# A fused pair of hybrid blocks on one core: the recurrence's keys made by another engine, and two chunks of the first mixer copied and turned earlier

## The chip, the cores and the metric

The kernel runs on 1 core of one Trainium2 chip. The metric is device time in microseconds (us) of one execution. Engines are TensorE (PE in the rows; PEld is its weight load), VectorE (DVE), ScalarE (ACT), GpSimd (POOL) and SyncE (SP), which issues the DMAs here.

## The reference, cut to what matters

A sequence of 256 tokens with 1024 features passes four layers, each of which is a feed-forward part, a mixer and a feed-forward part. Layers 0 and 1 have the first kind of mixer, layers 2 and 3 the second. Everything is float32.

```python
# mixer of layers 0 and 1: differential, stick-breaking and block attention
proj = h @ w_in
dq, dk = partial_rope(dq, cos, sin), partial_rope(dk, cos, sin)   # differential attention
p = softmax(causal(dq @ dk.T * scale)); w = p[:, :, 0] - lam * p[:, :, 1]

# mixer of layers 2 and 3: a gated recurrence and dilated window attention
hq, hf, hi, hg, ... = split(h @ w_in_2)
f = lb + (1.0 - lb) * sigmoid(hf)
q_a, k_a, v_a, log_f = silu(hq), 1.0 - f, hi, log(f)
# S_t = diag(f_t) S_{t-1} + k_t v_t^T ; o_t = S_t^T q_t
```

With s = sigmoid(hf), the keys are 1 - f = (lb - 1) * s + (1 - lb), and the logarithm is log((1 - lb) * s + lb).

## The kernel before, in words

**Weights.** All weights are streamed from HBM in units of 128 x 2048 numbers through three slots. SP loads a unit into `raw`, as two DMAs of 512 KB. ScalarE copies it to a rounded high half, `w_high` (`split_high`, L328); VectorE subtracts to get the low half, `w_low` (`split_low`, L333); TensorE multiplies three pairings of high and low parts (`product`, L371). A slot comes free when PE has used its unit, and `raw` when the low half is made.

**Order.** Each engine has a program written out by hand, one pass per unit `u`. In a mixer, ScalarE and VectorE split unit u + 2 while PE works on unit u, and each does the mixer's own small steps at named values of u, ahead of the split or behind it. Two units make one chunk of 512 projected columns in PSUM; behind the second, ScalarE copies the chunk out with the row's norm factor (L1233 in `mix1_act`, L1785 in `mix2_act`). PE does the small products of a unit in its "tail" (`mix1_tail`, `mix2_tail`).

**First mixer.** Chunks 0 and 1 are the queries and keys of the differential attention. At u = 2 and 4 ScalarE copies them to `stage`, VectorE rotates them (`rotated`, L1315 to L1318) and turns 32 x 32 squares (`squares_turned`, L898, into `sec_squares`), and SP brings the squares home by eight DMAs each (L920, at u = 8 and 10 of its program) into `dqT` and `dkT`. PE reads these in the tail of u = 6 (`causal_scores`, L957 to L963).

**Second mixer.** The chunks of q (silu) and f (sigmoid) of the recurrence come in two halves of four heads. They are turned in squares in the same way and land in `hland` (`hg_turned`), at u = 4 to 12. From there ScalarE copies `hqT` (L1791), takes the logarithm (L1802, four instructions, at u = 6 and 12; semaphore `lnf_done`), and VectorE makes the keys `kT` (`hkT` in the rows, L2028, four instructions, at u = 6 and 11; `k_done`) and scans the logarithm to a sum (L2040, at u = 6 and 13). The recurrence is then computed by doubling, in eight levels for each half of the heads, one level per unit from u = 9 (n = u - 9; level 0 of the first half at u = 9, level 3 at u = 12, level 4 at u = 13 in VectorE's and ScalarE's counts). For a level, POOL subtracts sums (L2118), ScalarE takes two exponentials (L1752, L1753), VectorE multiplies them with queries and keys (L1925, L1926, `q_late` and `decayed`), and PE multiplies these in its tail (L1647). Levels 1, 3 and 5 wait for PE together with the level behind them; so PE's tails of u = 11, 13 and 15 hold levels 1 and 2, 3 and 4, 5 and 6. The first lines of VectorE's part that makes the keys are

```python
dve.wait_ge(hT_in[1], at2(lay, 128, 64 * (hf + 1)))
for h in range(4):
    hd = 4 * hf + h
    a = nc.vector.tensor_scalar(kT[:, hd, :]..., hland[1][:, :, h]..., lbn[:, hd:hd + 1], omlb[:, hd:hd + 1], ALU.mult, ALU.add)
```

## Time and profile before

| | |
|---|---|
| median of 3 runs | 2657.8 us (2657.18 to 2657.87) |
| the profiled execution | 2656.82 us, its span 2655.0 us |
| DVE busy | 1967.1 us, 74% of the span |
| ACT busy | 1427.8 us, 54% |
| POOL busy | 166.1 us, 6% |
| granted TensorE clock | 1.00 over the span |
| HBM read | 478.02 MB, 180 GB/s over the span |

A row of a timeline gives the start in us from the span's start, the time to the end, the engine, the line, the operation, its output and inputs, and how many instructions are merged; in brackets the idle time ahead of it and what ended that. Instructions on one engine overlap by up to a tenth of a microsecond, so the step from start to start is what the next one sees.

### The profile page before, as it was taken

To read this page: it belongs to the slowest core of one execution; us is meant where nothing else is said; L and a number is where in the kernel's file an instruction comes from. 1 tells how busy PE (TensorE), PEld (TensorE's weight loads), DVE (VectorE), ACT (ScalarE), POOL (GpSimd) and SP (SyncE) were. 2 spreads that over 40 slices of the span, in tenths; PEclk is the share of its full clock that TensorE was granted. 3 is DMA by queue.
4 is the path that set the end of the run, shared out by engine and by line. 5 is a ranking of instruction groups with operands and counts; after the bars stand their busy time and mean duration, and the time that the engine had idled before them with its cause. 6 is when DMAs were issued, how large, how long until landed. Compare 5 with 4: busy or idle time off the path is not lost.

```text
span 2655.0 us, 42138 instructions
## 1 busy us (share of the span) xinstructions
PE 2645.1 (100%) x15660; PEld 2240.7 (84%) x15660; DVE 1967.1 (74%) x2660; ACT 1427.8 (54%) x2021; POOL 166.1 (6%) x98
## 2 busy tenths in 40 slices
PE   9999999999999999999999999999999999999999
PEld 8888888888888888888888888888888888888888
DVE  6777767777777876777776888567777769876676
ACT  5446565445446565544545767554454466765543
POOL 0000000000000000000000132000000012210000
PEclk9999999999999999999999999999999999999999
DMA  7556455655555545556555754546555665454553
GB/s 239 190 175 207 150 169 169 202 190 195 193 193 196 166 160 183 176 190 196 180 190 190 230 167 165 185 149 205 190 178 192 212 199 185 162 188 159 186 190 130
DMA packets 324380, 489.26 MB, mean 184 GB/s; under 512 B 17312, under 2 KB 204064, under 8 KB 324256
## 3 DMA queue, kind: packets, MB, share of 16 engines
q1 hardware_dynamic: 323968, 487.47, 56.0%
q8 instruction: 85, 1.39, 0.2%
q14 instruction: 39, 0.32, 0.0%
q10 hardware_dynamic: 288, 0.07, 0.0%
HBM read 478.02 MB, written 1.05 MB: 180 GB/s over the span
## 4 chain that ended last, share of the span: by engine, by line
PE 94%; DVE 2%; ACT 2%; issue 1%; DMA 0%; POOL 0%; SPq 0%; ACTq 0%; DVEq 0%
PE bank L371 48%; PE bank L573 22%; PE bank L571 12%; PE bank L476 5%; PE bank L941 2%; PE bank L984 1%; PE bank L390 1%; DVE w_low L333 1%; ACT w_high L328 0%; PE bank L976 0%; DVE log_decay L2040 0%; PE bank L1647 0%; POOL decay L2118 0%; PE bank L1167 0%; ACT log_decay L1802 0%
## 5 line engine op out<-in xcount | busy, mean ns | idle before, releaser
L333 DVE TENSOR_TENSOR w_low<-raw,w_high 128x2048 fp32r<-128x2048 f32 x435 | 1008.3, 2319 | 397.5 <-ACT w_high L328 397.1
L328 ACT ACTIVATE w_high<-raw 128x2048 fp32r<-128x2048 f32 x435 | 831.1, 1912 | 474.5 <-PE bank L571 243.0
L371 PE MATMUL bank<-w_high,xT_parts 128*128 128x512 f32 x2304 | 739.4, 395 | 0.0
L573 PE MATMUL bank<-xT_parts,w_high 128*128 128x512 f32 x2560 | 618.6, 391 | 0.0
L573 PEld LDWEIGHTS bank<-xT_parts,w_high 128*128 128x128 f32 x2560 | 472.1, 188 | 92.2
L371 PEld LDWEIGHTS bank<-w_high,xT_parts 128*128 128x128 f32 x2304 | 432.6, 188 | 89.9
L371 PE MATMUL bank<-w_low,xT_parts 128*128 128x512 f32 x1152 | 448.7, 389 | 0.0
L571 PEld LDWEIGHTS bank<-xT_parts,w_low 128*128 128x128 f32 x2560 | 334.5, 191 | 16.7
L571 PE MATMUL bank<-xT_parts,w_low 128*128 128x256 f32 x2560 | 339.4, 282 | 0.0
L668 ACT ACTIVATE siluT<-gateT 128x256 f32<-128x256 f32 x160 | 66.8, 417 | 407.3 <-DVE gateT L724 406.9
L371 PEld LDWEIGHTS bank<-w_low,xT_parts 128*128 128x128 f32 x1152 | 216.6, 188 | 42.6
L371 PE MATMUL bank<-w_high,hT_high 128*128 128x512 f32 x640 | 198.2, 391 | 0.0
L371 PE MATMUL bank<-w_low,hT_high 128*128 128x512 f32 x640 | 197.6, 390 | 0.0
L371 PE MATMUL bank<-w_high,hT_low 128*128 128x512 f32 x640 | 197.4, 390 | 0.0
L371 PEld LDWEIGHTS bank<-w_low,hT_high 128*128 128x128 f32 x640 | 120.2, 188 | 25.8
L371 PEld LDWEIGHTS bank<-w_high,hT_low 128*128 128x128 f32 x640 | 120.2, 188 | 25.5
L371 PEld LDWEIGHTS bank<-w_high,hT_high 128*128 128x128 f32 x640 | 115.1, 189 | 19.1
L476 PE MATMUL bank<-w_high,xT_parts 128*128 128x512 f32 x384 | 125.6, 398 | 0.9 <-DVE w_low L461 0.3
L715 DVE TENSOR_REDUCE gateT<-bank 128x256 f32<-128x512 f32 x160 | 109.3, 683 | 16.6 <-PE bank L571 16.6
L715 DVE TENSOR_REDUCE upT<-bank 128x256 f32<-128x512 f32 x160 | 109.3, 683 | 2.1 <-PE bank L571 2.1
L675 ACT ACTIVATE hT_high<-hiddenT 128x256 fp32r<-128x256 f32 x144 | 52.4, 410 | 64.0 <-PE bank L371 64.0
L476 PEld LDWEIGHTS bank<-w_high,xT_parts 128*128 128x128 f32 x384 | 71.9, 188 | 16.9 <-ACT w_high L422 1.2
(308 smaller groups left out, 2684.7 us busy)
## 6 DMA issues: line engine op xcount, KB each, us to landing
raw<-in_w_in SPq DMA_DIRECT2D x288, 512.0 KB, 4.6
raw<-in_ffn_w_in SPq DMA_DIRECT2D x176, 512.0 KB, 4.5
raw<-in_ffn_wd SPq DMA_DIRECT2D x88, 512.0 KB, 4.1
raw<-in_ffn_w_out SPq DMA_DIRECT2D x88, 512.0 KB, 4.1
raw<-in_ffn_wg SPq DMA_DIRECT2D x86, 512.0 KB, 3.8
raw<-in_ffn_wu SPq DMA_DIRECT2D x86, 512.0 KB, 4.7
raw<-in_w_out SPq DMA_DIRECT2D x32, 512.0 KB, 4.2
raw<-in_w_branch_a SPq DMA_DIRECT2D x16, 512.0 KB, 5.3
```

The source lines that it names most:

```text
L328: nc.scalar.activation(wh[slot][:], raw[slot][:], ACT.Copy).then_inc(high_done[slot], 1)
L333: nc.vector.tensor_tensor(wl[slot][:], raw[slot][:], wh[slot][:].bitcast(F32), ALU.subtract).then_inc(low_done[slot], 1)
L371: mm = pe.matmul(o[:, 0:n], x[:, rows], w[slot][:, col + j * n:col + (j + 1) * n], start=start and first, stop=stop and last)
L390: tr = pe.transpose(wk[2 * tt + g][:, k * P:(k + 1) * P], X[:, tt, kt * P:(kt + 1) * P], ident)
L476: return pe.matmul(out[tt][:], x[:, kt, tt * P:(tt + 1) * P], w[slot][:, halves(kt % 4)], start=start, stop=stop)
L571: mm = pe.matmul(bank[:, 0:SEQ], wl[s][:, w], xhl[:, kt, 0, :], start=False, stop=kt == KT - 1, skip_group_check=True)
L573: mm = pe.matmul(bank[:], wh[s][:, w], xhl[:, kt, :, :], start=kt == 0, stop=False, skip_group_check=True)
L668: nc.scalar.activation(sT[:, h, :], gT[:, h, :], ACT.Silu).then_inc(silT_done, 1)
L675: nc.scalar.activation(dst[:, k, :], hidT[:, k, :], ACT.Copy).then_inc(hTh_done, 1)
L715: return nc.vector.tensor_reduce(dst, bank[:].rearrange("p (a n) -> p n a", a=2), AX.X, ALU.add).then_inc(block_out, 1)
L941: mm = pe.matmul(o, w[slot][:, col], x[:, kt, :], start=first and kt == 0 and j % 2 == 0, stop=last and kt == KT - 1, skip_group_check=True)
L984: tr = pe.transpose(bank[:, k * SEQ + tt * P:k * SEQ + (tt + 1) * P], src[:, tt, (kt + k) * P:(kt + k + 1) * P], ident)
```

## The change

In the second mixer the keys are made by ScalarE, as `Identity` with a scale and a bias per partition, right behind the logarithm, at u = 6 and 12; VectorE's instructions go, and it waits for `k_done` at level 0. SP's wait for `lnf_done` goes. In the first mixer, at u = 2 and 4, ScalarE copies the chunk ahead of the high half of unit u + 2, and VectorE rotates and turns ahead of the low half; SP issues the squares at u = 7 and 9 instead of 8 and 10. The small steps at u = 1, 2 and 6 (`sq_head`, `rstd_row`) come ahead of the high half too.

```diff
--- before.py
+++ after.py
@@ -912,8 +912,8 @@
         def mix1_sp(sp, lay):
             for u in range(MIX1):
                 s = slot_of(u)
-                if u in (8, 10):
-                    si = u // 2 - 4
+                if u in (7, 9):
+                    si = (u - 7) // 2
                     sp.wait_ge(ssq_turned, at(lay, 2, si + 1))
                     for a in range(4):
                         for e in range(2):
@@ -1205,8 +1205,6 @@
                         if u == first + 6 + 4 * g:
                             act.wait_ge(pv_done, at(lay, NPV, n0 + 4 * g + 4))
                             nc.scalar.activation(oTh[b][:, 2 * g:2 * g + 2, :], wk[3][:].rearrange("p (k n) -> p k n", k=2), ACT.Copy).then_inc(oTh_done, 1)
-                if 0 < u < MIX1 - 1:
-                    split_high(act, 1, slot_of(u + 2), lay, mix_use(u + 2))
 
                 if u == 6:
                     act.wait_ge(rrow_done, at(lay, 1, 1))
@@ -1217,6 +1215,8 @@
                     rows = slice(HD * (1 - e), HD * (2 - e))
                     none = ident[rows, e * (P - 1):e * (P - 1) + 1]
                     nc.scalar.activation(sqh[rows, :, e, :], none.unsqueeze(2).broadcast_to((HD, 4, SEQ)), ACT.Copy).then_inc(zero_done, 1)
+                if 0 < u < MIX1 - 1 and u not in (2, 4):
+                    split_high(act, 1, slot_of(u + 2), lay, mix_use(u + 2))
                 c = u // 2 - 1
                 if u % 2 == 0 and 0 <= c < CH1 and c not in TURNED:
                     unit1_done(act, lay, u - 1)
@@ -1232,6 +1232,8 @@
                     for tt in range(TT):
                         a = nc.scalar.activation(dst[:, tt, :], acc[c % 2][tt][:], ACT.Copy, scale=rstd[:, tt:tt + 1])
                     a.then_inc(chunk_out, 1)
+                if u in (2, 4):
+                    split_high(act, 1, slot_of(u + 2), lay, mix_use(u + 2))
 
                 for first, n, i0, pv0 in ((DIFF0 + 2, NDI, 0, 0), (MOBA0 + 2, NMO, NDI, NDI + NSB)):
                     j = u - first
@@ -1405,6 +1407,11 @@
                     dve.wait_ge(oTh_done, at(lay, 6, i + 1))
                     nc.vector.scalar_tensor_tensor(oTl[0][:, 2 * i:2 * i + 2, :], wk[2][:].rearrange("p (k n) -> p k n", k=2), gdiff[:],
                                                    oTh[0][:, 2 * i:2 * i + 2, :].bitcast(F32), ALU.mult, ALU.subtract).then_inc(oTl_done, 1)
+                if u in (2, 4):
+                    si = u // 2 - 1
+                    rotated(dve, lay, si)
+                    dve.wait_ge(rope_done, at(lay, 4, si + 1))
+                    squares_turned(stage[si], ssq[si]).then_inc(ssq_turned, 1)
                 if 0 < u < MIX1 - 1:
                     split_low(dve, 1, slot_of(u + 2), lay, mix_use(u + 2))
 
@@ -1452,12 +1459,6 @@
                     nc.vector.tensor_tensor(nlam[:], nlam[:], cols[:, C1_LAM0:C1_LAM0 + 1], ALU.subtract)
                     link(dve, nc.vector.tensor_tensor(gdiff[:], cols[:, C1_DIFF:C1_DIFF + 1], cols[:, C1_LAM1:C1_LAM1 + 1], ALU.mult))
 
-                if u in (2, 4):
-                    si = u // 2 - 1
-                    rotated(dve, lay, si)
-                    dve.wait_ge(rope_done, at(lay, 4, si + 1))
-                    squares_turned(stage[si], ssq[si]).then_inc(ssq_turned, 1)
-
                 if u == 12:
                     dve.wait_ge(osq_done, at(lay, 1, 1))
                     link(dve, nc.vector.tensor_reduce(ssd[:], osq[:].rearrange("p t (h d) -> p (t h) d", d=P), AX.X, ALU.add))
@@ -1523,7 +1524,6 @@
                         sp.wait_ge(hq_out, at2(lay, 2, 1))
                     if c == 3:
                         sp.wait_ge(k_done, at2(lay, 2, 1))
-                        sp.wait_ge(lnf_done, at2(lay, 2, 1))
                     squares_home(sp, hsq[c % 2], hland[c % 2], hT_in[c % 2])
                 if u == 33:
                     sp.wait_ge(apow_done, at2(lay, 6, ATT_GROUPS))
@@ -1803,6 +1803,12 @@
                                                      hland[1][:, :, h].rearrange("p k t j -> p t k j"), ACT.Ln,
                                                      bias=lb[:, hd:hd + 1], scale=omlb[:, hd:hd + 1])
                         a.then_inc(lnf_done, 1)
+                        for h in range(4):
+                            hd = 4 * hf + h
+                            a = nc.scalar.activation(kT[:, hd, :].rearrange("p (t k j) -> p t k j", t=TT, k=4),
+                                                     hland[1][:, :, h].rearrange("p k t j -> p t k j"), ACT.Identity,
+                                                     bias=omlb[:, hd:hd + 1], scale=lbn[:, hd:hd + 1])
+                        a.then_inc(k_done, 1)
 
                 for hf, step, b0 in ((0, HG0 + LEVELS + 1, 2), (1, HG0 + NHG + 1, 0)):
                     if u == step:
@@ -1907,6 +1913,7 @@
                     hs = slice(4 * hf, 4 * hf + 4)
                     if lev == 0:
                         dve.wait_ge(hq_out, at2(lay, 2, hf + 1))
+                        dve.wait_ge(k_done, at2(lay, 2, hf + 1))
                         if hf == 0:
                             link(dve, nc.vector.memset(att[:], 0.0))
                     dve.wait_ge(dec_done, at2(lay, NHG, n + 1))
@@ -2022,14 +2029,7 @@
 
                 for hf, step, scan in ((0, 6, 6), (1, 11, 13)):
                     if u == step:
-                        dve.wait_ge(hT_in[1], at2(lay, 128, 64 * (hf + 1)))
-                        for h in range(4):
-                            hd = 4 * hf + h
-                            a = nc.vector.tensor_scalar(kT[:, hd, :].rearrange("p (t k j) -> p t k j", t=TT, k=4),
-                                                        hland[1][:, :, h].rearrange("p k t j -> p t k j"),
-                                                        lbn[:, hd:hd + 1], omlb[:, hd:hd + 1], ALU.mult, ALU.add)
                         nc.vector.memset(gc[:, 4 * hf:4 * hf + 4, P:P + 1], 0.0)
-                        a.then_inc(k_done, 1)
                     if u == scan:
                         dve.wait_ge(lnf_done, at2(lay, 2, hf + 1))
                         if hf == 0:
```

ScalarE in the second mixer, from the exponentials of level 3 (L1752, L1753) past the second half's logarithm (L1802) to the high half of unit 15; L1785 copies a chunk. Before:

```order
L1752 ACTIVATE decay<-decay 128x64x8
L1753 ACTIVATE decay<-decay 128x64x8
L328 ACTIVATE w_high<-raw 128x2048
L1785 ACTIVATE hg_v<-bank,rstd 128x512 x2
L1802 ACTIVATE log_decay<-hg_turned_121,lb,one_minus_lb 128x2x128 x4
L1752 ACTIVATE decay<-decay 128x32x16
L1753 ACTIVATE decay<-decay 128x32x16
L328 ACTIVATE w_high<-raw 128x2048
```

Now:

```order
L1752 ACTIVATE decay<-decay 128x64x8
L1753 ACTIVATE decay<-decay 128x64x8
L328 ACTIVATE w_high<-raw 128x2048
L1785 ACTIVATE hg_v<-bank,rstd 128x512 x2
L1802 ACTIVATE log_decay<-hg_turned_121,lb,one_minus_lb 128x2x128 x4
L1808 ACTIVATE hkT<-hg_turned_121,one_minus_lb,lb_minus_one 128x256 x4
L1752 ACTIVATE decay<-decay 128x32x16
L1753 ACTIVATE decay<-decay 128x32x16
L328 ACTIVATE w_high<-raw 128x2048
```

The four key instructions (L1808) stand between the logarithm and the next level's exponentials, which the next high half follows. `mix2_dve` has no L2028 any more, neither here nor at u = 6.

VectorE in the first mixer, from the low halves behind the query chunk to those behind the turning of the key chunk (`sec_squares_71`); L333 is the low half. Before:

```order
L333 TENSOR_TENSOR w_low<-raw,w_high 128x2048 x2
L1451 TENSOR_TENSOR neg_lam<-lam_exp 128x1
L1452 TENSOR_TENSOR neg_lam<-neg_lam,cols 128x1
L1453 TENSOR_TENSOR gain_diff<-cols 128x1
L1315 TENSOR_TENSOR rope_t_101<-stage_69,kblk 128x128
L1315 TENSOR_TENSOR rope_t_102<-stage_69,kblk 128x128
L1315 TENSOR_TENSOR rope_t_103<-stage_69,kblk 128x128
L1315 TENSOR_TENSOR rope_t_104<-stage_69,kblk 128x128
L1317 TENSOR_TENSOR stage_69<-rope_t_101,rope_t_102 128x16x8
L1318 TENSOR_TENSOR stage_69<-rope_t_103,rope_t_104 128x16x8
L898 STREAM_TRANSPOSE sec_squares_71<-stage_69 128x2x4x4x32
L333 TENSOR_TENSOR w_low<-raw,w_high 128x2048 x2
```

Now:

```order
L333 TENSOR_TENSOR w_low<-raw,w_high 128x2048 x2
L1317 TENSOR_TENSOR rope_t_101<-stage_69,kblk 128x128
L1317 TENSOR_TENSOR rope_t_102<-stage_69,kblk 128x128
L1317 TENSOR_TENSOR rope_t_103<-stage_69,kblk 128x128
L1317 TENSOR_TENSOR rope_t_104<-stage_69,kblk 128x128
L1319 TENSOR_TENSOR stage_69<-rope_t_101,rope_t_102 128x16x8
L1320 TENSOR_TENSOR stage_69<-rope_t_103,rope_t_104 128x16x8
L898 STREAM_TRANSPOSE sec_squares_71<-stage_69 128x2x4x4x32
L333 TENSOR_TENSOR w_low<-raw,w_high 128x2048
L1458 TENSOR_TENSOR neg_lam<-lam_exp 128x1
L1459 TENSOR_TENSOR neg_lam<-neg_lam,cols 128x1
```

Both engines' splits of unit 6 now follow the key chunk's steps: on VectorE one of the two low halves ahead of the rotation and the three small lambda steps came behind the turn.

SP in the first mixer (L909 loads a unit's half, L920 brings squares home), one piece of the difference:

```order
-L909 DMA raw<-in_w_in 128x2x512 x16
+L909 DMA raw<-in_w_in 128x2x512 x14
 L920 DMA dqT<-sec_squares_70 64x1x256 x8
 L909 DMA raw<-in_w_in 128x2x512 x4
 L920 DMA dkT<-sec_squares_71 64x1x256 x8
-L909 DMA raw<-in_w_in 128x2x512 x40
+L909 DMA raw<-in_w_in 128x2x512 x42
```

The squares are issued one unit, that is two loads, earlier in SP's queue.

## Rows read from the trace of the kernel before

**Rows 1.** The page: busy time, share of the span and instructions of the engines.
```profile
PE 2645.1 (100%) x15660; PEld 2240.7 (84%) x15660; DVE 1967.1 (74%) x2660; ACT 1427.8 (54%) x2021; POOL 166.1 (6%) x98
```

**Rows 2.** Waits of PE over the whole span: total us, times, longest us.
```profile
PE bank L1647 <- DVE decayed L1926: 3.3, 3, 1.6
...
PE bank L957 <- DMA dkT<-sec_squares: 0.7, 1, 0.7
```

**Rows 3.** Timeline of ACT, mixer of layer 2, units 12 and 13: start us, us.
```profile
1516.57 0.64 ACT L1752 ACTIVATE decay<-decay 128x512 f32<-128x512 f32 x1 [5.20 <-POOL decay L2118]
...
1520.58 2.07 ACT L1802 ACTIVATE log_decay<-hg_turned,lb,one_minus_lb 128x256 f32<-128x256 f32 x4
1522.55 0.62 ACT L1752 ACTIVATE decay<-decay 128x512 f32<-128x512 f32 x1
...
1523.59 1.91 ACT L328 ACTIVATE w_high<-raw 128x2048 fp32r<-128x2048 f32 x1
```

**Rows 4.** Timeline of DVE, the same stretch.
```profile
1512.42 2.28 DVE L333 TENSOR_TENSOR w_low<-raw,w_high 128x2048 fp32r<-128x2048 f32 x1
1514.62 3.04 DVE L2028 TENSOR_SCALAR hkT<-hg_turned,lb_minus_one,one_minus_lb 128x256 f32<-128x256 f32 x4
...
1517.77 0.42 DVE L1925 TENSOR_TENSOR q_late_first<-decay,hqT 128x256 f32<-128x256 f32 x1
...
1523.72 0.43 DVE L1925 TENSOR_TENSOR q_late<-decay,hqT 128x256 f32<-128x256 f32 x1 [0.30 <-ACT decay L1753]
...
1524.74 0.42 DVE L1926 TENSOR_TENSOR decayed<-decay,hkT 128x256 f32<-128x256 f32 x1
1525.53 3.78 DVE L333 TENSOR_TENSOR w_low<-raw,w_high 128x2048 fp32r<-128x2048 f32 x1 [0.37 <-ACT w_high L328]
...
1538.25 0.41 DVE L1926 TENSOR_TENSOR decayed<-decay,hkT 128x256 f32<-128x256 f32 x1
```

**Rows 5.** Timeline of POOL, the same stretch.
```profile
1506.47 1.90 POOL L2118 TENSOR_TENSOR decay<-log_decay 128x1024 f32<-128x1024 f32 x1 [3.57 <-DVE decayed_first L1926]
1512.58 3.96 POOL L2118 TENSOR_TENSOR decay<-log_decay 128x1024 f32<-128x1024 f32 x1 [4.21 <-DVE decayed L1926]
```

**Rows 6.** Timeline of PE: the tails of units 13 and 15.
```profile
1525.30 0.43 PE L1647 MATMUL bank<-q_late_first,decayed_first 128*32 128x32 f32 x29
...
1538.81 0.69 PE L1647 MATMUL bank<-q_late_first,decayed_first 128*64 128x64 f32 x16 [1.55 <-DVE decayed L1926]
```

**Rows 7.** Timeline of ACT, the same mixer, unit 8.
```profile
1490.47 1.92 ACT L328 ACTIVATE w_high<-raw 128x2048 fp32r<-128x2048 f32 x1 [1.18 <-PE bank L371]
...
1495.82 1.06 ACT L1791 ACTIVATE hqT<-hg_turned 128x1024 f32<-128x1024 f32 x1 [0.85 <-DMA hg_turned<-hg_squares]
```

**Rows 8.** Chain that ended last, mixer of layer 0: start us, us.
```profile
227.16 1.26 DVE sec_squares L898
...
228.43 0.55 SPq L920
...
233.24 3.08 DMA dkT<-sec_squares
```

**Rows 9.** The DMA issues of the turned squares, all layers: ns min/median/max.
```profile
L920 SPq DMA_DIRECT2D dkT<-sec_squares x16: 542/600/1560, 228.4 to 858.8; - x16
```

**Rows 10.** Timeline of ACT, mixer of layer 0, units 3 to 7.
```profile
218.89 3.72 ACT L328 ACTIVATE w_high<-raw 128x2048 fp32r<-128x2048 f32 x2 [3.83 <-PE bank L371]
222.51 1.24 ACT L1233 ACTIVATE stage<-bank,rstd 128x512 f32<-128x512 f32 x2
...
230.00 1.91 ACT L328 ACTIVATE w_high<-raw 128x2048 fp32r<-128x2048 f32 x1 [3.76 <-PE bank L371]
...
235.75 1.91 ACT L328 ACTIVATE w_high<-raw 128x2048 fp32r<-128x2048 f32 x1 [2.41 <-PE bank L941]
```

**Rows 11.** Timeline of DVE, mixer of layer 0, unit 2.
```profile
213.00 2.29 DVE L333 TENSOR_TENSOR w_low<-raw,w_high 128x2048 fp32r<-128x2048 f32 x1 [0.73 <-ACT w_high L328]
```

**Rows 12.** The page: DMA issues, KB each, median us from issue to landing.
```profile
raw<-in_w_in SPq DMA_DIRECT2D x288, 512.0 KB, 4.6
```

## The prediction, made before the changed kernel ran

> **What bounds the kernel now.** I read the page first: TensorE (PE) is busy for 2645.1 us of the span of 2655.0 us [rows 1], so everything outside its matmuls is worth 9.9 us at most, and only what makes PE wait counts. Then PE's waits: two are of size [rows 2]. At line 1647 it waits for VectorE's `decayed` (key tiles multiplied by a decay): 3.3 us in three times, the longest 1.6 us. At line 957 it waits once, 0.7 us, for the DMA that brings home the turned K squares. The first lies in the recurrence of layers 2 and 3, the second in the first mixer of layer 0. The change touches the work ahead of both. So I read the timelines of ACT (ScalarE), DVE (VectorE), POOL and PE there [rows 3 to 6], to see who releases whom. The mixers of layers 2 and 3 repeat each other, so I work one out and double it.
>
> How small a difference can be told: the three runs lie within 0.7 us, and I count over 0.2% (5.3 us) as faster or slower.
>
> **Recurrence, second half of the heads (unit 12).** Removed from VectorE: four key instructions, 3.04 us at 1514.62 [rows 4]. Added to ScalarE: four instructions of the same shape behind the logarithm. The trace has no such Identity, so I bound it. Below: 1.06 us, the copy of the same number of elements (128x1024) in one instruction [rows 7]. Above: 3.04 us, what the keys took on VectorE. The nearest row by far is the logarithm itself, which has the same input, shape and two per-partition operands: its four start at 1520.58 and the next instruction at 1522.55 [rows 3], so 1.97 us. I take 1.97 us.
>
> What VectorE gains here: nothing. Its next work is level 3 at 1517.77 [rows 4], which needs ScalarE's exponentials of level 3. They start at 1516.57, when POOL's subtraction ends, and the last ends at about 1517.7 [rows 3, 5]. The keys filled a gap.
>
> What ScalarE's extra 1.97 us costs: all of it. In ScalarE's queue the exponentials of level 4 stand right behind (1522.55), without idle, then the high half of unit 15 (1523.59) [rows 3]. VectorE's level 4 waits for these exponentials (0.30 us at 1523.72) and is done at 1525.16; its low half of unit 15 then waits for the high half (0.37 us at 1525.53) [rows 4]. PE takes level 4 at 1525.30 [rows 6], with no time in hand. So PE is held by 1.97 us at the tail of unit 13.
>
> Does the old wait at the tail of unit 15 shrink by that, since PE comes later? It is 1.55 us at 1538.81 [rows 6], on VectorE's level 6, done at 1538.66 [rows 4]. From 1525.53 VectorE works through without idle to there, so level 6 shifts by 1.97 us too, and the old wait stays. Net: +1.97 us per layer, **+3.94 us** for two.
>
> One rule bears on this. POOL's subtraction of level 3 took 3.96 us and the one of level 1 took 1.90 us [rows 5]; the keys took 3.04 us beside it. The Trainium skill, "SBUF — State Buffer", "SBUF: two separate sides", says that VectorE and GpSimd share one port pair as an exclusive lock, which whoever starts first keeps for a whole instruction. By that rule POOL stood behind the low half (1512.42 to 1514.70 [rows 4]) and the keys behind POOL, so that taking the keys away gives POOL nothing; the sum stays at +3.94 us. If both were slowed by sharing instead, it would be the first rival below.
>
> **Recurrence, first half (unit 6).** ScalarE again gets 1.97 us. Up to the copy `hqT`, which the decay levels need, it idles 1.18 us and 0.85 us [rows 7], together 2.03 us, the second for a DMA that does not move. So 1.97 us just fit: 0. With the cover gone, a microsecond more passes to the levels. The scan on VectorE waits for the logarithm, which is still ahead of the keys; nothing is gained there either. The SP wait that goes (`lnf_done`) is implied by `k_done`, later on the same engine: 0. VectorE's new wait for `k_done` at level 0 is on work some 10 us old: 0.
>
> **First mixer, units 2 and 4.** ScalarE copies the chunk ahead of the high half: at 218.89 it runs two high halves (3.72 us), then the copy at 222.51 [rows 10]. Now the copy starts one high half sooner, by 1.8 us. VectorE rotates and turns ahead of the low half (2.2 us, the pace of [rows 11]) and ahead of the small lambda steps (about 0.4 us): the turn at 227.16 [rows 8] comes about 2.6 us sooner. The eight SP issues take 4.8 us (228.43 to 233.24), and the last lands 3.08 us later, at 236.32 [rows 8]. All this moves to about 233.7, PE comes at 236.32 - 0.7 = 235.6, and the wait is gone: **-0.7 us**, in layer 0 only, for layer 1 shows none. The profiled execution had one issue of 1560 ns against a median of 600 [rows 9]; without it there is no wait to win, so this term lies between -0.7 and 0.
>
> What becomes late: the low half of unit 6 ends at about 228, and PE starts unit 6 at 230.0 [rows 10]: 2 us in hand. The low half of unit 4 ended at 215.3 [rows 11] and comes 1.9 us later, against unit 4's start at 218.8 [rows 10]. On SP the eight issues now stand ahead of the load of unit 9: issued at about 230.7 and landed 4.6 us later [rows 12], at 235.3, against its use at 235.75 [rows 10]. A little late costs nothing, since its low half is due 15 us later. The sq_head and rstd_row steps fill idle time: 0.
>
> **Sum.** Profiled execution: 2656.82 us (span and 1.8 us around it) + 3.94 - 0.7 = 2660.1. It lies 1.0 us under the median of 2657.8, to which I add the same: **2661.0 us**, 0.12% longer. With the bounds of the key price: at 1.06 us it is 2659.2; at 3.04 us the first half no longer fits (1.01 us over), (3.04 + 1.01) x 2 = 8.1, 2665.2.
>
> **Rivals.**
> - *POOL was slowed by the keys.* Then its subtraction ends up to 2.06 us sooner (3.96 - 1.90), ScalarE's block of unit 12 starts so much sooner, and this cancels the 1.97 us: 2657.8 - 0.2 - 0.7 = 2656.9. Against it: VectorE was in a low half until 1514.70, and from there 1.9 us is the whole subtraction [rows 4, 5]. Chance 0.10.
> - *Faster: VectorE is the bound of the levels.* 3.04 us less on it removes both long waits at line 1647, about 3.1 us in two layers: 2657.8 - 3.1 - 0.7 = 2654.0. It decides if VectorE comes to level 4 with work still queued. Against it: both idle gaps of [rows 4] name ScalarE. Chance 0.06.
> - *The waits overlap.* Had VectorE slack between the tails, PE's delay at unit 13 would eat the 1.55 us: (1.97 - 1.55) x 2 = 0.8, 2657.9. Against it: no idle there. Chance 0.07.
> - *Slower by over 0.2%.* The first half of the keys has 0.06 us in hand. From 2.03 us for four instructions on, the excess is paid in both halves: at 2.5 us it gives (2.5 + 0.47) x 2 = 5.9, 2663.0, and up to 2665.2 at the upper bound. A table load between the logarithm and the Identity would be worse. Chance 0.10.
> - *As forecast*, 2659 to 2662: 0.67.
>
> The Trainium skill, "ScalarE: Activation LUTs", "Table sets: the hidden batching unit", has identity in every table set, so it sees no such load; no row here shows an Identity in this set.
>
> **Numbers.** The range 2656.8 to 2663.5 leaves out the second rival and the upper part of the fourth. Faster than 2652.5 needs more than all waits that the change touches: 0.02. Slower than 2663.1: 0.09. Within: 0.89.
>
> **What would show it.** Line 1808 on ScalarE: 16 instructions, four in 1.97 us. VectorE idle at about 1514.7, POOL's subtraction still 3.96 us. PE's waits at line 1647 up from 3.3 to about 7.2 us, with a new one of about 2 us at the tail of unit 13 and the old 1.55 us kept; the wait at line 957 gone. Wrong would be: POOL at 1.9 us, no wait at unit 13, or `hqT` without idle before it.

## The result, and the profile after

The changed kernel took 2663.57 us (median of 11 runs, 2662.97 to 2666.09) against 2657.77 us (2656.92 to 2659.1, 11 runs) of the kernel before: 5.8 us more, ratio 1.0023, 95% interval 1.0014 to 1.0032. The forecast was 3.2 us more, 2661.0, and within 0.2%; 2663.57 lies just outside its range (to 2663.5) and just beyond 0.2%.

The profiled execution took 2663.22 us. The page's head, with PE's row that answers to [rows 1]:

```profile
span 2661.4 us, 42142 instructions
...
PE 2647.5 (99%) x15660; PEld 2241.5 (84%) x15660; DVE 1958.6 (74%) x2644; ACT 1435.2 (54%) x2037; POOL 166.1 (6%) x98
```

VectorE has 16 instructions less and 8.5 us less to do, ScalarE 16 and 7.4 us more: the keys of both layers. The span is 6.4 us longer. Where? PE passes the last transpose (L390) ahead of each mixer and each feed-forward part in the same order in both kernels, so the start of that row can be compared stretch by stretch, in us after minus before: start of the program +0.47; mixers of layers 0 to 3: +0.90, +0.57, +1.98, +1.95; last feed-forward part +0.36; all others together +0.15.

**The recurrence** (layer 2 shown). ScalarE's timeline at unit 12, beside [rows 3]:

```profile
1522.61 2.07 ACT L1802 ACTIVATE log_decay<-hg_turned,lb,one_minus_lb 128x256 f32<-128x256 f32 x4
1524.58 2.07 ACT L1808 ACTIVATE hkT<-hg_turned,one_minus_lb,lb_minus_one 128x256 f32<-128x256 f32 x4
1526.54 0.63 ACT L1752 ACTIVATE decay<-decay 128x512 f32<-128x512 f32 x1
```

The keys take 1.96 us from start to start (1524.58 to 1526.54), like the logarithm ahead of them, and the exponentials of level 4 stand behind. VectorE and POOL in the same stretch, beside [rows 4, 5]:

```profile
1519.79 0.42 DVE L1932 TENSOR_TENSOR q_late_first<-decay,hqT 128x256 f32<-128x256 f32 x1 [3.05 <-ACT decay L1753]
...
1527.72 0.43 DVE L1932 TENSOR_TENSOR q_late<-decay,hqT 128x256 f32<-128x256 f32 x1 [2.26 <-ACT decay L1753]
```
```profile
1514.60 3.97 POOL L2118 TENSOR_TENSOR decay<-log_decay 128x1024 f32<-128x1024 f32 x1 [4.21 <-DVE decayed L1933]
```

Where VectorE made keys it now idles for 3.05 us; POOL's subtraction is as long without them (3.97 us, before 3.96); and VectorE's wait ahead of level 4 is 2.26 us for 0.30. PE at the tails of units 13 and 15, in layer 2 and in layer 3, beside [rows 6]:

```profile
1529.30 0.59 PE L1647 MATMUL bank<-q_late_first,decayed_first 128*32 128x32 f32 x30 [2.10 <-DVE decayed L1933]
...
1542.80 0.69 PE L1647 MATMUL bank<-q_late_first,decayed_first 128*64 128x64 f32 x16 [0.16 <-DVE decayed L1933]
...
2227.23 0.43 PE L1647 MATMUL bank<-q_late_first,decayed_first 128*32 128x32 f32 x29 [2.17 <-DVE decayed L1933]
...
2240.74 0.69 PE L1647 MATMUL bank<-q_late_first,decayed_first 128*64 128x64 f32 x16 [1.57 <-DVE decayed L1933]
```

The new wait at unit 13 is there in both. The old one at unit 15 is there in layer 3 (1.57 us) and nearly gone in layer 2, though the layers cost the same. The table of stretches of layer 2 (length, busy time of PE, PEld, DVE, ACT and POOL, granted clock, DMA share, GB/s) says why:

```profile
1520.00:1527.00 7.00, 7.00 (x32) 5.63 (x30) 5.43 (x9) 7.00 (x12) 1.96 (x1) 1.00 0.25 73
...
1529.30:1531.00 1.70, 1.70 (x66) 1.54 (x67) 1.48 (x1) 0.19 (x1) 1.70 (x1) 0.53 0.38 146
1531.00:1533.00 2.00, 2.00 (x7) 1.58 (x6) 2.00 (x1) 1.81 (x3) 0.16 (x1) 0.54 0.05 12
1533.00:1535.00 2.00, 2.00 (x10) 1.61 (x9) 2.00 (x7) 2.00 (x3) 0.00 (x0) 1.00 0.37 35
```

Behind its idle stretch of 2.10 us PE is granted half its clock for about 3.4 us, so it comes some 1.4 us later to unit 15 (a wait of 0.16 us there for the 1.57 of layer 3) and finds VectorE nearly done. VectorE sets the time of unit 15 in both layers, so the slow clock took the place of a wait and cost nothing more.

The keys of the first half (unit 6) hold nothing up. No table load stands between logarithm and keys there or at unit 12, and `hqT`, ahead of which ScalarE idled for 0.85 us [rows 7], still has idle time ahead of it in layer 2 (0.27 us in layer 3):

```profile
1497.83 1.06 ACT L1791 ACTIVATE hqT<-hg_turned 128x1024 f32<-128x1024 f32 x1 [0.17 <-DMA hg_turned<-hg_squares]
```

**The first mixer** (layer 0 shown), beside [rows 8, 10]. SP, ScalarE, VectorE and PE from 226 us on:

```profile
226.43 5.38 SPq L920 DMA_DIRECT2D dkT<-sec_squares  x8
231.85 5.54 SPq L909 DMA_DIRECT2D raw<-in_w_in  x6
```
```profile
238.78 1.91 ACT L328 ACTIVATE w_high<-raw 128x2048 fp32r<-128x2048 f32 x1 [3.48 <-DMA raw<-in_w_in]
240.60 0.39 ACT L1255 ACTIVATE expd<-masked,neg_max 128x128 f32<-128x128 f32 x1
```
```profile
238.66 0.68 DVE L1374 TENSOR_REDUCE neg_max<-masked 128x2 f32<-128x512 f32 x1
240.72 2.29 DVE L333 TENSOR_TENSOR w_low<-raw,w_high 128x2048 fp32r<-128x2048 f32 x1 [1.38 <-ACT w_high L328]
...
243.39 0.75 DVE L1426 SCALAR_TENSOR_TENSOR w_diff<-expd,ratio_lam,expd 128x128 f32<-128x128 f32 x2
```
```profile
244.20 0.55 PE L1107 MATMUL bank<-konst,w_diff 128*128 128x128 f32 x3 [1.28 <-DVE w_diff L1426]
```

The turn is early and PE's wait at L957 is gone. But the load of unit 9 and the eight issues have changed places. Before, SP issued that load ahead of them (the last two of the four DMAs in the first row):

```profile
223.19 3.04 SPq L909 DMA_DIRECT2D raw<-in_w_in  x4
228.43 6.37 SPq L920 DMA_DIRECT2D dkT<-sec_squares  x8
```

Now SP begins it behind the eight issues, at 231.85. Its high half can't start before 238.78 on ScalarE, and stands ahead of the first head's exponentials, whose input was ready at 239.34 (238.66 + 0.68). On VectorE the low half stands ahead of `w_diff` in the same way. So PE waits 1.28 us for `w_diff` (L1107).

A second, smaller thing at unit 1 of the same mixer, on ScalarE:

```profile
208.34 1.06 ACT L1217 ACTIVATE sq_head<-konst 64x1024 f32<-64x1024 f32 x1 [0.88 <-POOL rstd L554]
209.42 1.92 ACT L328 ACTIVATE w_high<-raw 128x2048 fp32r<-128x2048 f32 x1
```

The diff also sets `sq_head` ahead of the high half of unit 3. It starts there as ScalarE's first work of the mixer, which waits for `rstd`; the high half starts at 209.42 against 208.03 before, and VectorE's low half at 211.37 against 209.98 (0.5 us of each difference is there before the mixer begins).

### The profile page after: what moved, and what is told of

Read it like the earlier page. It is cut to its first block, busy times and chain, and to the rows that moved or that the text cites. A ratio compares the mean times of both kernels' runs of the same rounds, so it can differ in the third digit from the quotient of the medians.

```text
span 2661.4 us, 42142 instructions
## 1 busy us (share of the span) xinstructions
PE 2647.5 (99%) x15660; PEld 2241.5 (84%) x15660; DVE 1958.6 (74%) x2644; ACT 1435.2 (54%) x2037; POOL 166.1 (6%) x98
## 4 chain that ended last, share of the span: by engine, by line
PE 93%; DVE 3%; ACT 2%; issue 1%; DMA 1%; SPq 1%; POOL 0%; DVEq 0%; ACTq 0%
PE bank L371 48%; PE bank L573 22%; PE bank L571 11%; PE bank L476 5%; PE bank L984 1%; DVE w_low L333 1%; PE bank L941 1%; PE bank L390 1%; ACT w_high L328 1%; DMA raw<-in_w_in 0%; PE bank L976 0%; DVE log_decay L2040 0%; SPq L920 0%; PE bank L1647 0%; POOL decay L2118 0%
## 5 line engine op out<-in xcount | busy, mean ns | idle before, releaser
L333 DVE TENSOR_TENSOR w_low<-raw,w_high 128x2048 fp32r<-128x2048 f32 x435 | 1008.4, 2319 | 402.2 <-ACT w_high L328 401.8
```

The costliest lines, as they stand in the source:

```text
L333: nc.vector.tensor_tensor(wl[slot][:], raw[slot][:], wh[slot][:].bitcast(F32), ALU.subtract).then_inc(low_done[slot], 1)
```

## The experiments

Each kernel was timed in 11 runs (e7 in 10) beside the kernel before. The table gives the difference of the medians, and from each profiled execution the differences in us against the profile of before, stretch by stretch as above. Bold: stretches that the kernel edits.

| kernel | medians | ratio, 95% interval | start | mixer 0 | mixer 1 | mixer 2 | mixer 3 | last part |
|---|---|---|---|---|---|---|---|---|
| e1 keys only | +4.7 | 1.0017 (1.0008 to 1.0026) | +0.34 | -0.18 | +0.46 | **+1.98** | **+2.36** | +0.35 |
| e2 first mixer only | +2.3 | 1.0007 (0.9998 to 1.0016) | +0.76 | **+1.12** | **+0.94** | +0.02 | +0.44 | -0.01 |
| e3 e2, SP as before | +1.8 | 1.0007 (0.9998 to 1.0016) | -0.12 | **+0.37** | **+0.75** | +0.59 | +0.57 | -0.01 |
| e4 keys late | +0.6 | 1.0002 (0.9993 to 1.0011) | +0.80 | -0.45 | +0.02 | **+0.04** | **+0.22** | +0.35 |
| e5 log and scan early | -0.8 | 0.9997 (0.9988 to 1.0006) | 0.00 | -0.06 | +0.03 | **-0.63** | **-0.15** | +0.37 |
| e6 the same, keys on VectorE | -1.8 | 0.9994 (0.9985 to 1.0003) | -0.27 | +0.23 | +0.47 | **-0.64** | **+0.01** | 0.00 |
| e7 SP only | +6.8 | 1.0026 (1.0016 to 1.0035) | +0.38 | **+5.26** | **+4.49** | +0.03 | -0.04 | -0.02 |
| e8 e2, unit 9 behind the head | +0.3 | 1.0001 (0.9992 to 1.0010) | +0.39 | **-0.18** | **+0.68** | +0.01 | +0.36 | +0.03 |
| e9 e8, high halves back | -0.4 | 0.9998 (0.9989 to 1.0007) | +0.69 | **-0.40** | **+0.41** | +0.01 | +0.28 | -0.03 |
| e10 scan split | -2.1 | 0.9993 (0.9984 to 1.0002) | -0.40 | -0.34 | -0.01 | **-1.24** | **-0.75** | +0.36 |
| e11 the same, keys on VectorE | -1.7 | 0.9995 (0.9986 to 1.0004) | +0.46 | -0.35 | -0.01 | **-0.74** | **-0.20** | +0.03 |
| e12 e11 and e9 | -1.8 | 0.9994 (0.9985 to 1.0003) | 0.00 | **-0.40** | **+0.41** | **-0.71** | **-0.71** | -0.02 |
| e13 e10 and e9 | -1.8 | 0.9993 (0.9984 to 1.0002) | +0.31 | **-0.41** | **+0.42** | **-1.25** | **-0.80** | +0.34 |
| e14 e10 and memsets | -2.3 | 0.9992 (0.9983 to 1.0001) | +0.27 | +0.18 | +0.43 | **-1.27** | **-0.54** | 0.00 |

The plain numbers show what one execution differs from another where nothing was edited: -0.40 to +0.80 at the start, -0.45 to +0.23 and -0.01 to +0.47 in the first two mixers, -0.04 to +0.59 in the last two. So nothing shows that the changed kernel's +0.47 at the start is an effect of the change, and a single stretch tells nothing under half a microsecond. The intervals are about as coarse for the medians: only those of the changed kernel, e1 and e7 leave out 1, so for every other kernel the medians alone do not show that it is faster or slower than before.

### The two parts apart

**e1** moves only the keys:

```diff
  # mix2_act, behind the logarithm of u = 6 and 12
+ for h in range(4): a = nc.scalar.activation(kT..., hland[1]..., ACT.Identity, bias=omlb..., scale=lbn...)
+ a.then_inc(k_done, 1)
  # mix2_dve
- for h in range(4): a = nc.vector.tensor_scalar(kT..., ...)
```

> The kernel before with the recurrence's keys alone moved to ScalarE, behind the logarithm of the same step; the first mixer is that of before. Theory (the recurrence term was right and the first mixer's was not): the scan of the second half starts 1.96 us later in each of the two layers, so 3.9 us over before, with a VectorE idle of 3.0 us before the scan and a TensorE wait of 2.1 us at the end of unit 13, as in the changed kernel's layer 2. Rival (the first mixer and the program's start and end make all of the loss beyond noise): under 3 us. Rival (the recurrence part costs more than its four instructions): over 5 us.

Measured +4.7 us; the mixers +1.98 and +2.36, and +0.35 in the last part. The recurrence's term holds; neither rival does. In layer 3 PE waited 2.59 us at unit 13, not 2.1, and its clock fell behind that (last section).

**e2** has only the first mixer's part of the diff.

> The kernel before with the first mixer's part of the change alone; the keys stay on VectorE. Theory (the load of unit 9 stands on SP behind the eight transfers of the K squares, lands late, and its high half stands on ScalarE ahead of the exponentials of the first heads; the heads' sum of squares stands ahead of a high half): +0.9 us in layer 0's mixer and +0.6 in layer 1's, so 1.0 to 1.9 us over before, with TensorE waiting about 1.3 us for the weights' difference of the softmax in layer 0. The step of the prediction that this tries says -0.7 to 0.

Measured +2.3 us, mixers +1.12 and +0.94; PE waits 1.5 and 0.5 us for `w_diff`. More than expected, and of the other sign than the prediction's -0.7, though the interval of the medians just holds 1; it is the new waits that show the sign. The two parts alone add up to 7.0 us where the change has 5.8, a microsecond that I can't assign and that lies within the intervals.

**e3** is e2 with one thing back:

```diff
-                if u in (7, 9):
-                    si = (u - 7) // 2
+                if u in (8, 10):
+                    si = u // 2 - 4
```

> The first mixer's part alone, as in the last, but the transfers of the squares are issued at units 8 and 10 as before, so that the loads of units 7 to 9 stand ahead of them on SP. Theory (the late load makes the wait): TensorE's wait of 1.3 us for the weights' difference is gone, the load of unit 9 lands in under 5 us, and the time is within -0.4 to +0.6 us of before; what is left over is 0.2 us a layer of the sum of squares ahead of the high half. Rival (the early turning on VectorE makes the wait, whenever the squares travel): still +1.0 to +1.9.

The wait for `w_diff` is gone, as the theory has it, but the time is +1.8 us, outside what was expected. Two reasons stand in the profile. First, PE's waits at L957 are back, 0.9 and 0.5 us: turned early but sent late, the squares land late, so the early turn alone gains nothing. Second, +0.59 and +0.57 us in mixers that the kernel doesn't edit, with a wait of 0.65 us at unit 13 where the profile of before has none. That tail has no slack [rows 6]; e2's profile, also with unedited mixers, has 0.17 us there and 0.70 in layer 3, where before has 0.15. So the second is no more than executions differ by, and explains this one execution but not the median, whose interval holds 1: what the kernel costs beyond the first stays open.

**e7** is the kernel before with only the SP edit (8, 10 to 7, 9). VectorE turns late, so SP stands at the wait with the load of unit 9 behind it.

> The kernel before, with the transfers of the squares issued at units 7 and 9 and nothing else: VectorE turns the keys' squares as late as before (228.4 us in layer 0), so SyncE now holds the load of unit 9 behind a wait and the eight transfers, until about 234.8 us, some 2.7 us later than in the first-mixer-only kernel. Theory (the late load of unit 9, whose high half stands ahead of the first head's exponentials, makes the wait for the weights' difference): that wait grows from 1.5 to 3.5 to 4.5 us in layer 0 and to some 3 us in layer 1, and the wait for the turned keys stays at 0.7: 4 to 7 us over before. Rival (the early turning on VectorE or the order of the high halves makes it): under 1 us over before.

Measured +6.8 us. SP and PE in layer 0:

```profile
228.81 5.36 SPq L920 DMA_DIRECT2D dkT<-sec_squares  x8
234.22 3.80 SPq L909 DMA_DIRECT2D raw<-in_w_in  x6
```
```profile
245.83 0.90 PE L1107 MATMUL bank<-konst,w_diff 128*128 128x128 f32 x3 [3.06 <-DVE w_diff L1419]
```

A load that is 2.4 us later (234.22 for 231.85) makes the wait 1.8 us longer (3.06 for 1.28): the load sets it, not VectorE's order, which is that of before here. The waits are 3.1 and 2.8 us, less than expected, and the wait at L957, expected to stay, is gone; the stretches, +5.26 and +4.49, are longer than the waits. This execution lies 2.8 us above the kernel's median, so they overstate the usual cost. The difference is the clock again:

```profile
240.00:243.00 3.00, 2.77 (x24) 2.57 (x22) 0.64 (x1) 2.59 (x4) 0.00 (x0) 1.00 1.05 388
...
246.00:248.00 2.00, 2.00 (x52) 1.61 (x53) 0.00 (x0) 0.49 (x1) 0.00 (x0) 0.50 0.94 331
248.00:250.00 2.00, 2.00 (x10) 2.00 (x11) 1.72 (x4) 0.00 (x0) 0.00 (x0) 0.50 0.49 184
250.00:252.00 2.00, 2.00 (x11) 2.00 (x11) 2.00 (x2) 1.66 (x7) 0.00 (x0) 0.50 0.00 0
```

### The order in the queue of the first mixer

**e8** keeps the late load of e2 and moves who stands ahead of whom:

```diff
-                if 0 < u < MIX1 - 1 and u not in (2, 4):
+                if 0 < u < MIX1 - 1 and u not in (2, 4, 7):
                     split_high(act, 1, slot_of(u + 2), lay, mix_use(u + 2))
  # behind the head's exponentials (ScalarE); VectorE the same behind w_diff, with split_low
+                if u == 7:
+                    split_high(act, 1, slot_of(u + 2), lay, mix_use(u + 2))
```

> The first-mixer part alone, as it is in the change, but both halves of unit 9's weights stand behind the first head's exponentials (ScalarE) and weights' difference (VectorE) instead of ahead of them; the load of unit 9 is as late as there. Theory (it costs because its high half stands ahead of that head): TensorE's wait of 1.5 and 0.5 us for the weights' difference is gone, as is that of 0.7 us for the turned keys: 0 to 1 us under before, 2 to 3 us under the first-mixer-only kernel. Rival (the late load hurts whoever needs it, unit 9 on TensorE itself): the wait moves to unit 9's first matmul and the time stays 1 to 2.5 us over before.

+0.3 us, so 2.0 us under e2 with the same late load, though not under before as hoped. The waits of 1.5 and 0.5 us for head 0 and those at L957 are gone; in their place head 1 waits 0.20 us. So the waits came from the place in the queue.

**e9** also puts the high halves of all units but 4, 6 and 9 back ahead of `rstd_row` and `sq_head`.

> As the last one of the first mixer (unit 9's halves behind the first head), and the high halves of all units but 4, 6 and 9 back ahead of ScalarE's small copies, as before the change. Theory (in the change the zeroing copy of the branch's queries at unit 1 waits for its turn ahead of the high half of unit 3, and VectorE's low half of unit 3 comes late): the waits of TensorE in units 2 and 3 go, 0.2 us in each layer, so 0.3 to 0.6 us under the last kernel and 0.2 to 1.0 under before. Rival (units 2 and 3 are as long as in the last kernel): no difference from it.

-0.4 us, 0.7 under e8 when each is taken against the kernel before beside it, 0.5 by the two stretches: in the direction and about the size expected, but less than the runs tell apart. Against before the ratio is 0.9998: all repairs together make the first mixer's part worth nothing that can be measured. In layer 0 it gains 0.40 us, but three of seven kernels with the old first mixer show that without it: PE's wait at L957 is 0.2, 0.3, 0.3, 0.6, 0.7, 0.7, 0.9 and 0.9 us in the eight profiles that have that mixer as before (before itself, e1, e4, e5, e6, e10, e11, e14). The 0.7 of the one profile [rows 2] was never a fixed price. In layer 1 e9, e12 and e13 all show +0.41, of which 0.20 is head 1's wait.

### What the keys may cost, and where

**e4** moves the second half's four instructions from unit 12 to unit 14 of ScalarE's program, where it was idle.

> The recurrence's keys on ScalarE as in the first, but those of the second half issued at unit 14, behind that step's copy and scaled row, where ScalarE is idle for some 3.9 us, and no longer between the logarithm and the row scaled at unit 12. Theory (only the place of the second half's four instructions costs): the 3.9 us are gone, within -0.5 to +0.6 us of before. Rival (VectorE, freed of 1.94 us of keys a half, was the bound): 3 us under before. Rival (keys on ScalarE cost wherever they stand): +2 to +4 us.

+0.6 us, the mixers +0.04 and +0.22. The same four instructions on the same engine cost 2 us at unit 12 and nothing at unit 14. The rival in which VectorE is the bound would have shown here: it has the keys off and gains nothing.

**e5** asks what the old wait of 1.55 us at unit 15 hangs on:

```diff
-                for hf, step in ((0, 6), (1, 12)):       # ScalarE: logarithm
+                for hf, step in ((0, 6), (1, 11)):
-                for hf, step, scan in ((0, 6, 6), (1, 11, 13)):   # VectorE
+                for hf, step, scan in ((0, 6, 6), (1, 11, 11)):
  # keys of the second half: ScalarE, u = 12
```

> The kernel before with the keys on ScalarE, and the second half's logarithm one unit earlier (unit 11, in ScalarE's idle stretch of 5.2 us), its scan on VectorE at unit 11 (in the idle stretch of 3.0 us that the keys left there) and its keys on ScalarE at unit 12, where the logarithm stood. Theory (what ends last in the second half is the scan at unit 13, ahead of the level products whose lateness is the TensorE wait of 1.55 us at unit 15; the keys were only ever as dear as what stood behind them): that wait goes in both layers, 1.0 to 1.6 us each, so 2 to 3.2 us under before. Rival (GpSimd's subtraction of 3.96 us at unit 11 is slowed by the scan beside it, and the level products behind it come late): 0 to +3 us. Rival (the wait at unit 15 comes from somewhere else): within 0.5 us of before.

-0.8 us, where 2 to 3.2 were expected. The wait at unit 15 fell from 1.55 to 0.19 us in both layers, as the theory said, but a new one of 0.90 and 1.43 us stands at unit 13. POOL and VectorE in layer 2:

```profile
1512.53 3.96 POOL L2127 TENSOR_TENSOR decay<-log_decay 128x1024 f32<-128x1024 f32 x1 [4.21 <-DVE decayed L1942]
...
1525.97 3.92 POOL L2127 TENSOR_TENSOR decay<-log_decay 128x1024 f32<-128x1024 f32 x1 [3.62 <-DVE decayed L1942]
```
```profile
1512.35 2.29 DVE L333 TENSOR_TENSOR w_low<-raw,w_high 128x2048 fp32r<-128x2048 f32 x1
1514.57 2.21 DVE L2049 TENSOR_TENSOR_SCAN log_decay<-ones,log_decay 128x128 f32<-128x128 f32 x1
...
1525.81 2.28 DVE L333 TENSOR_TENSOR w_low<-raw,w_high 128x2048 fp32r<-128x2048 f32 x1
```

The first scan took 2.21 us and the next seven 2.29 together. It could not run until the subtraction ended at 1516.49. The subtraction, 1.9 us when alone, had itself stood behind the low half, which started 0.18 us sooner. At 1525.97 POOL again comes 0.16 us behind a low half and takes 3.92 us. In [rows 4] it was the other way round: the low half came later than POOL and took 3.78 us for 2.28. Whoever starts first keeps the other out for the whole instruction, and both are done 4.08 us after the first began, in either order (1525.81 to 1529.89 here, 1525.23 to 1529.31 in [rows 4, 5]). That is the exclusive lock of the Trainium skill ("SBUF — State Buffer", "SBUF: two separate sides"); these rows agree with it, for the scan too.

**e6** puts the keys on VectorE at unit 13 instead, with e5's logarithm and scan, and nothing on ScalarE.

> The keys stay on VectorE, those of the second half at unit 13 where the scan was, and the logarithm (ScalarE) and the scan (VectorE) of the second half stand at unit 11; ScalarE gets no new work. Theory: at unit 13 VectorE now does 1.94 us of keys for 2.62 us of scan, so the wait at unit 15 shrinks by some 0.7 us a layer: 1.0 to 1.8 us under before. If this gains as much as the last kernel or more, moving the keys to ScalarE had no part in the gain. Rival (GpSimd slowed by the scan): slower than before.

-1.8 us by the medians (its profiled execution, 2656.57 us, lies 1.1 us above its median). It gains no less than e5, by medians and by stretches, so nothing shows that the keys' engine has a part in that gain.

**e10** runs four of the eight scan instructions at unit 11 and four at unit 13, with e5's keys:

```diff
-                        for h in range(4):
+                        for h in range(4 if hf == 0 else 2):
+                if u == 13:
+                    for h in range(2, 4): ... tensor_tensor_scan ...
```

> The kernel with logarithm and scan at unit 11 and the keys on ScalarE at unit 12, but only the first four of the second half's eight scan instructions at unit 11; the other four at unit 13, where all of them were. Theory (a scan instruction cannot run while GpSimd's subtraction runs: the first one took 2.21 us for 0.33, until that subtraction had ended, so the eight end 0.8 us too late; four of them end in time, and at unit 13 the other four fit behind GpSimd's second long subtraction): the TensorE wait of 0.9 and 1.43 us at unit 13 goes, that at unit 15 stays under 0.5, so 2.0 to 3.2 us under before, some 1.5 to 2 under the kernel with all eight at unit 11. Rival (what is late at unit 13 is the logarithm or the exponentials on ScalarE): no change from that kernel.

-2.1 us, at the low end of what was expected, and 1.3 under e5 (1.5 to 2 expected). PE's waits in the recurrence, which were 3.3 us before [rows 2]:

```profile
PE bank L1646 <- DVE decayed L1942: 1.3, 3, 0.7
```

The wait at unit 13 is gone in layer 2 and 0.69 us in layer 3, that at unit 15 is 0.3 us in both.

**e11** is e10's split with the keys on VectorE.

> The same split of the scan, with the keys left on VectorE, at unit 13 ahead of the four scan instructions. Theory (the keys' instruction on VectorE runs beside GpSimd's subtraction without either slowing, so at unit 13 it fills the time in which scan and subtraction exclude each other): 2.0 to 3.4 us under before, no slower than with the keys on ScalarE. Rival (1.94 us more on VectorE at unit 13 come out as a longer wait at unit 15): 1 to 2 us slower than with the keys on ScalarE.

-1.7 us, short of the 2.0 expected, and 0.4 behind e10, which the runs don't tell apart. Its wait at unit 15 is 1.06 and 1.26 us where e10 has 0.3: part of its rival is true. The keys do not run freely beside the subtraction: the four took 2.99 us there (1.94 was expected), and 3.04 us in [rows 4]. In e10 the subtraction began ahead of the low half (1524.44 to 1524.74), in e11 behind it.

**e12** and **e13** join e9's first mixer to e11 and e10.

> The split scan with the keys on VectorE, together with the first mixer of the kernel that sets unit 9's halves behind the first head and the high halves back. The sum of the two, if the stages don't touch each other: 2.4 to 4.2 us under before. If it is nearer to 2, the first mixer's part is worth nothing.

> The split scan with the keys on ScalarE, together with the first mixer that sets unit 9's halves behind the first head. If the stages add: the 2.1 us of the split scan and the 0.35 us of that mixer, 2.0 to 3.0 us under before. Rival (they don't add, as in the last pair, where the sum was no better than its recurrence part alone): 1.7 to 2.1 under before.

Both -1.8 us, where 2.4 to 4.2 and 2.0 to 3.0 were expected of the sums: the first mixer adds nothing to either. The stages do add (mixers 0 and 1 as in e9, 2 and 3 as in e10 and e11), but -0.41 and +0.42 cancel.

### The last feed-forward part

Six kernels with the keys on ScalarE (the changed one, e1, e4, e5, e10, e13) lose 0.34 to 0.37 us there, and none of the kernels with the keys on VectorE does. VectorE's timeline of the changed kernel has it between two of its own instructions:

```profile
2650.32 0.42 DVE L734 TENSOR_TENSOR hiddenT<-siluT,upT 128x256 f32<-128x256 f32 x1 [0.46 <-DVE siluT L731]
```

**e14** is e10 with four memsets of one column more in each half, which restores VectorE's count of instructions.

> The split scan with the keys on ScalarE, and on VectorE four memsets of one column more in each half, so that VectorE has as many instructions as before. Theory (the last FFN is 0.36 us longer because the place of VectorE's instructions in its stream has shifted, and their fetch falls elsewhere): VectorE's idle of 0.46 us ahead of hiddenT in the last FFN is gone, 0.1 to 0.4 us under the same kernel without the memsets. Rival (it comes from ScalarE's longer stream or from the keys): the idle stays.

The idle is gone from the last part, and so is the loss there. But it is not gone from the kernel: it turns up in another feed-forward part, at

```profile
1943.32 0.42 DVE L734 TENSOR_TENSOR hiddenT<-siluT,upT 128x256 f32<-128x256 f32 x1 [0.46 <-DVE siluT L731]
```

Of the 160 such instructions a gap of 0.46 us stands ahead of one in the kernel before (at 478.6 us) and in every kernel with the keys on VectorE, and ahead of two in each with the keys on ScalarE, e14 too (first at 479.1 us). So the memsets moved the second gap but didn't remove it, although VectorE has as many instructions as before again. Its place hangs on VectorE's instructions ahead of it; why there is a second one stays open, and that it is a fetch of instructions is only argued. The 0.2 us by which e14's median lies under e10's is within the spread of the runs.

## Why the prediction was right or wrong

- **Recurrence, second half, +1.97 us a layer: right.** Measured +1.98 and +1.95. The price by the logarithm's row held (1.96 us), as did the chain from ScalarE through VectorE to PE, and VectorE's gain of nothing; e1 shows it alone, and e4 that it is the place that costs.
- **The old wait at unit 15 kept: right for the cost, half right in the trace.** It is 1.57 us in layer 3. In layer 2 the reduced clock took its place, so PE's waits at L1647 sum to 6.0 us, not the 7.2 that I named as a sign.
- **First half, 0: right.** The mixers cost no more than the second half's keys, and `hqT` keeps 0.17 and 0.27 us of idle time ahead of it.
- **The rivals.** POOL slowed by the keys: fallen, 3.97 us without them. VectorE the bound: fallen, in e4 it has the keys off and gains nothing. Overlapping waits: fallen, 1.57 us kept in layer 3. The case slower by over 0.2% came about, but not by its mechanism: the keys cost 1.96 us each time, not 2.5, and there is no table load.
- **First mixer, -0.7 us: wrong in sign, and this is the step that failed.** It measured +0.90 and +0.57 us, about +1.5 together, 2.2 us from the forecast; the sum missed by 2.6. Layer 0 carries the finding: the 0.71 us wait went as forecast, but one of 1.28 us came. In layer 1 the new wait is 0.15 us, and most of the +0.57 is no more than what unedited mixers differ by. Two of its sentences failed. "A little late costs nothing, since its low half is due 15 us later": I asked when the late thing's own product is used, and not what stands behind it in ScalarE's and VectorE's queues. Head 0 stood there. The load was also later than I put it: SP began it at 231.85, not at 230.7, and the high half started at 238.78, not at 235.3 (0.5 us of each is the program's later start). For the 4.6 us to landing are a median of single DMAs, and a unit is two, the second issued behind the first; why it landed only at 238.8 is not shown. e7 (later still: worse) and e8 (same load, other place: repaired) show it. "The sq_head and rstd_row steps fill idle time: 0": the first `sq_head` is ScalarE's first work that waits for `rstd`, and took the high half of unit 3 with it; by the stretches of e8 and e9 about 0.5 us in the two layers, which the runs don't tell apart from 0.
- **The gain itself** was read off one execution. Over eight profiles the wait at L957 is 0.2 to 0.9 us, so the lower bound that I gave, with one long DMA issue as the reason, was sensible, but the change traded it for a wait of 1.28 us, 1.49 in e2.
- **Not in the sum:** +0.36 us in the last feed-forward part, at a gap whose cause is open. The start's +0.47 is what executions differ by.

## What to carry to other kernels

When an edit makes something late, price it by whoever stands behind it in each in-order queue, not by when its own product is due. A move is worth what its old and new places hold: the same four instructions cost 2 us at unit 12 and nothing at unit 14, and the best order found (e10, 2.1 us under before, though its interval of 0.9984 to 1.0002 still holds 1) came mainly from moving logarithm and scan: e11, with the keys still on VectorE, has 1.7 of it. A wait read off one execution is a sample; look whether its neighbour layer shows it before taking it as a gain.

## What the runs showed of the hardware

**A short idle of TensorE can halve its clock.** Behind a wait of 2.10 us in the changed kernel's layer 2 the granted clock was 0.53 and 0.54 (the lower of its two levels, 1.2 of 2.4 GHz) for about 3.4 us; behind 2.59 us in e1's layer 3 (next rows) and 2.76 us in e7's layer 1 it was 0.50 for as long, and behind 3.06 us in e7's layer 0 for nearly 7 us. Behind 2.17 us in the changed kernel's layer 3 and 2.07 us in e1's layer 2 it stayed at 1.00. So near 2.1 us it went both ways here. In the one profiled execution of e7 the waits of 3.06 and 2.76 us came with mixers 5.26 and 4.49 us longer; in the changed kernel's layer 2 the slow clock cost nothing more, since PE would have waited at unit 15 anyway.

```profile
2226.30 0.43 PE L1646 MATMUL bank<-q_late_first,decayed_first 128*32 128x32 f32 x29 [2.59 <-DVE decayed L1932]
```
```profile
2226.00:2228.00 2.00, 1.70 (x66) 1.56 (x67) 1.63 (x2) 0.50 (x1) 1.76 (x1) 0.67 0.42 162
2228.00:2230.00 2.00, 2.00 (x6) 1.52 (x6) 2.00 (x1) 1.80 (x3) 0.16 (x1) 0.50 0.00 0
```

**Tenths of a microsecond decide a microsecond.** Which of VectorE's low half and POOL's subtraction starts first, 0.16 us apart in e5 and 0.30 in e10, decides which of the two takes 3.8 to 3.9 us.

**A gap of 0.46 us between two instructions of VectorE** that need nothing else stands at 1 or 2 of 160 places. The second moved from the last feed-forward part (e10) to an earlier one (e14) when only 16 small memsets were added; its cause is open.
